# Two expert rows per token, weighted and summed by products with diagonal matrices in PSUM instead of by two vector instructions

## The chip, the cores and the metric

The kernel runs on one core of one Trainium2 chip. The metric is the device time of the core in microseconds (us), from the program's start to its end; less is better. The core has five engines that run their own instruction streams and meet at semaphores: PE (TensorE, matrix products into PSUM), DVE (VectorE), ACT (ScalarE), POOL (GpSimd) and SP (SyncE, which here only starts transfers). The DMA engines move data between HBM and SBUF.

## What is computed

One inference step of a network with two layers, for 128 context tokens and 256 latent tokens of width 1024. Each layer has three kinds of attention heads after one input projection, an output projection and a layer norm, and then a mixture of experts, to which the change belongs. Each token is sent to two of 32 experts, and the two results are added with two weights of that token:

```python
def hier_moe(h, router_group, router_expert, w_gate, w_up, w_down):
    ...
    top_w = jax.nn.softmax(top_v, axis=-1) * g_w
    expert_id = g_sel[:, None] * EXPERTS_PER_GROUP + top_i
    gates = jnp.sum(jax.nn.one_hot(expert_id, N_EXPERTS, dtype=jnp.float32) * top_w[..., None], axis=1).astype(h.dtype)
    ...
    y = jnp.einsum('nef,efd->nd', jax.nn.silu(a) * u * gates[:, :, None], w_down)
    return y.reshape(B, T, D)

def post_norm_residual(x, y, gate, w, b):
    return layer_norm(ALPHA * x + gate * y, w, b)
```

All data are float32.

## The kernel before

The 384 tokens are three tiles of 128 tokens (TILES = 3; tile 0 is the context, tiles 1 and 2 are the latent tokens), with the tokens on the partitions. Each engine runs one hand-written program; a loop over the two layers l holds the stages, and the order of an engine's work is the order of its code.

The expert stage of a layer goes over 16 pairs of experts. For a pair, POOL fetches the rows of its tokens with an indirect DMA (`fetch`, L2154), PE multiplies them with the gate and up weights (L1194) and the down weights (L1218), and POOL scatters the resulting rows to a table `rows` in HBM (`scatter`, L2160; the trace calls it expert_rows). The row of a token's first expert and that of its second stand side by side in the table. Expert pairs with over 64 tokens for one expert need one more round, an "item"; in layer 0 there is one (L1247 to L1283 on PE, L2172 for its scatter), in layer 1 there is none.

When all rows are stored, ACT starts one transfer for each tile (L1583), which brings both rows of the tile's 128 tokens into `gath[t]`, 128 partitions x 2 x 1024. Then DVE does for each tile in turn (L2096 to L2107): three instructions that make (a * w0 + b * w1) * gate2 out of the two rows a and b, the token's two weights `wts[:, 0, t]` and `wts[:, 1, t]` and the row gate2; one that adds ALPHA * x; the moments of the layer norm (L1797, L1803, L1804); and the two instructions of the norm, L1811 and L1813, with the inverse root by POOL (L2147) between them. The end of L1813 signals `ln2_done`.

Who waits for that: in layer 1, the last one, SP stores each tile when its `ln2_done` comes (L840), and the kernel ends with the third store. In layer 0, PE goes on with the next layer's input projection. Its first jobs are, for each tile, 8 transposes of x (L910), which wait for the tile's `ln2_done`, and, after ACT or DVE has copied them out (L1415, L1607), 24 products of 256 columns (L922). SP reloads the attention bias into the buffer of gate2 once all three tiles have their `ln2_done` (L760), and POOL masks it (L2131, L2136).

The weights `wts` come from `weights` on DVE (L1900 to L1907), at the start of the expert stage, before the first of the pairs. The buffer `decay`, 128 partitions x 6 x 128, holds the decay tables of the retention heads; nothing reads it from the retention scores of a layer to the tables of the next. In the expert stage PE writes PSUM banks 0 to 7; the last rows leave banks 5 and 6 with L1493 and L1988 (for an item L1507 and L2019). `ident` is a 128 x 128 identity matrix in SBUF.

Of the kernel before, what the change touches and what calls it, by code (L numbers as in the profile page):

```python
# [22 lines left out]
ALU = mybir.AluOpType  # L23
# [9 lines left out]
TILES = TOKENS // P  # L33
# [351 lines left out]
def build(nc, x_prompt, x_sample, c, cache_na_k, cache_na_v, state_ret, cache_diff_k, cache_diff_v, c_ctx,  # L385
# [12 lines left out]
    with ExitStack() as ctx:  # L398
# [3 lines left out]
        def signal(name, step=0, start=0):  # L402
            s = Signal(ctx.enter_context(nc.semaphore(name)), step, start)
            if start:
                started.append(s)
            return s
# [24 lines left out]
        decay = sb("decay", [P, RET_HEADS, P])  # L431
# [13 lines left out]
        ps = ctx.enter_context(nc.psum_tensor("ps", [P, 8, 512], F32))  # L445

        ident = kc[:, K_ID:K_ID + P]
# [31 lines left out]
        gate2 = [bias[:, :, :, :].rearrange("p h r c -> p (h r c)")[:, k * D:(k + 1) * D] for k in range(2)]  # L479
# [13 lines left out]
        gath = [at(i, 2, D) for i in GATH]  # L493
# [7 lines left out]
        wts = route(2, TILES)  # L501
# [6 lines left out]
        gst = route(8, TILES)  # L508
# [35 lines left out]
        gathered = [signal(f"gathered{i}", 16) for i in range(TILES)]  # L544
# [65 lines left out]
        o_out, o_stored = signal("o_out", 16), signal("o_stored", 1, start=1)  # L610
        var2, rstd2, ln2_done = signal("var2", TILES), signal("rstd2", TILES), signal("ln2_done", TILES)
        combined = signal("combined", TILES)

        dve_link = signal("dve_link", DVE_LINKS)
        pool_link = signal("pool_link", POOL_LINKS)
# [230 lines left out]
        def _(pe):  # L846
# [395 lines left out]
            def item(l, o0, i):  # L1242
# [42 lines left out]
                                           start=(j == 0), stop=(j == 1))  # L1285
                mm.then_inc(o_down.sem, 1)

            for l in range(DEPTH):
                pe.wait_ge(row_act.sem, row_act.at(l, 0))
                pe.wait_ge(row_dve.sem, row_dve.at(l, 0))  # L1290
                for kind, i in FRONT:
                    if l == 0 and kind == "job" and i == JOB_NO["pN", 0, 0]:
                        early_mods(0, 0, CH)
                        early_columns(0)
                    if kind == "job":
                        front_job(l, i)
                    elif kind == "att":
                        if i < N_ATT:
                            scores(l, i)
                        if N_DIFF + 1 < i <= N_ATT:  # L1300
                            probs_T(l, i - 1)
                        if i >= 2:
                            values(l, i - 2)
                        if 1 <= i <= N_DIFF + 1:
                            probs_T(l, i - 1)
                    elif kind == "states":
                        ret_states(l)
                    elif kind == "scores":
                        ret_scores(l, i)
                    elif kind == "out":  # L1310
                        ret_out(l, i)
                mix_T(l, 0)
                mix_T(l, 1)
                out_proj(l, 0)
                mix_T(l, 2)
                out_proj(l, 1)
                rows_logits(l, 0)
                if l + 1 < DEPTH:
                    early_mods(l + 1, 0, 4)
                out_proj(l, 2)  # L1320
                rows_logits(l, 1)
                if l + 1 < DEPTH:
                    early_mods(l + 1, 4, CH)
                rank_products(l, 0, True)
                rows_logits(l, 2)
                if l + 1 < DEPTH:
                    early_columns(l + 1)
                rank_products(l, 1, True)
                rank_products(l, 1, False)
                rank_products(l, 2, True)  # L1330
                first_places(l, (0, 1))
                rank_products(l, 2, False)
                first_places(l, (2,))
                totals(l)
                experts(l)
                wait_alone(pe, items_known, items_known.at(l, 1))
                o1 = items_before(pe, l + 1)
                o0 = items_before(pe, l)
                with pe.If(o1 > o0):
                    with pe.Fori(o0, o1) as i:  # L1340
                        item(l, o0, i)
                pe.wait_ge(row_act.sem, row_act.at(l, PAIRS))
                pe.wait_ge(row_dve.sem, row_dve.at(l, PAIRS))
                pe.wait_ge(o_act.sem, o_act.at(o1, 0))
                pe.wait_ge(o_dve.sem, o_dve.at(o1, 0))

        def drain_to(kind, what, where):

# [239 lines left out]
        def _(dve):  # L1588
# [311 lines left out]
            def weights(l, chain):  # L1900

                dve.wait_ge(gexp_done.sem, gexp_done.at(l, 1))
                chain.link(dve.tensor_reduce(gst[:, 3, :], gtmp, AX.X, ALU.add))
                chain.link(dve.tensor_scalar(gst[:, 5, :], gst[:, 4, :], 1.0, None, ALU.add))
                chain.link(dve.tensor_tensor(gst[:, 5, :], gst[:, 5, :], gst[:, 3, :], ALU.mult))
                chain.link(dve.reciprocal(wts[:, 0, :], gst[:, 5, :]))
                chain.link(dve.tensor_tensor(wts[:, 1, :], wts[:, 0, :], gst[:, 4, :], ALU.mult))  # L1907

            def most(l, chain):

# [110 lines left out]
            for l in range(DEPTH):  # L2021
# [72 lines left out]
                    with dve.Fori(o0, o1) as i:  # L2094
                        item(l, o0, i)
                for t in range(TILES):  # L2096
                    dve.wait_ge(gathered[t].sem, gathered[t].at(l, 16))
                    a, b = gath[t][:, 0, :], gath[t][:, 1, :]
                    if t == 0:
                        dve.wait_ge(gate2_in.sem, gate2_in.at(l, gate2_in.step))  # L2100
                    chain.link(dve.tensor_scalar(a, a, wts[:, 0, t:t + 1], None, ALU.mult))
                    chain.link(dve.scalar_tensor_tensor(a, b, wts[:, 1, t:t + 1], a, ALU.mult, ALU.add))
                    dve.tensor_tensor(a, a, gate2[min(t, 1)], ALU.mult).then_inc(combined.sem, 1)
                    dve.wait_ge(combined.sem, combined.at(l, t + 1))
                    chain.link(dve.scalar_tensor_tensor(x[:, t, :], x[:, t, :], ALPHA, a, ALU.mult, ALU.add))
                    moments(t, chain, var2)
                    normalise(l, t, chain)  # L2107
# [3 lines left out]
        def _(pool):  # L2111
# [37 lines left out]
            def fetch(l, i):  # L2149

                wait_alone(pool, idx_known, idx_known.at(l, 1 if i == 0 else i // GPAIRS + 2))
                if i >= 2:
                    wait_alone(pool, xt_ready, xt_ready.at(l, 2 * (i - 2) + 2))
                pool.indirect_dma_start(xr[i % 2], None, h2d, bass.IndirectOffsetOnAxis(ap=idxu[:, 2 * i + 1:2 * i + 2], axis=0),  # L2154
                                        bounds_check=TOKENS, oob_is_err=False).then_inc(xr_in[i % 2].sem, 16)
# [21 lines left out]
            for l in range(DEPTH):  # L2177
# [48 lines left out]
                wait_alone(pool, h2_stored, h2_stored.at(l, h2_stored.step))  # L2226
                for i in range(4):
                    fetch(l, i)
                for i in range(PAIRS):
                    if i + 4 < PAIRS:  # L2230
                        fetch(l, i + 4)
                    scatter(l, i)
# [10 lines left out]

DVE_LINKS = 205
POOL_LINKS = 19

_INS = ['x_prompt', 'x_sample', 'c', 'cache_na_k', 'cache_na_v', 'state_ret', 'cache_diff_k', 'cache_diff_v', 'c_ctx',
# [24 lines left out]
```

## Times and profile of the kernel before

| what | us |
| --- | --- |
| median of 3 runs | 1266.61 (1263.4 to 1271.74) |
| the profiled execution, its own time | 1269.94 |
| span of its trace | 1268.0 |
| PE busy with products | 1063.1 (84%) |
| DVE busy | 431.6 (34%) |
| ACT busy | 209.4 (17%) |
| POOL busy | 179.3 (14%) |
| last tile's two rows gathered to the end of its norm, see the rows below | 1252.99 to 1262.42 |

The views that are read are the page (a summary of one profiled execution), the chain of work that ended last, the instructions in order of time with merged neighbours, the groups of instructions by line, and tables of stretches with the busy time of each engine and the clock that was granted to TensorE (1.00 is its full 2.4 GHz, 0.50 is 1.2 GHz). A float32 product of the program stands in the trace as two recorded matmuls (the 24 products of L922 for one tile are 48 records); a transpose is one record.

### The profile page before, as it was taken

Reading aid. Unit: us, or ns where it says so; the run is one execution under the profiler, and the core shown is the slowest. Engines: PE = TensorE matmul, PEld = TensorE weight load, DVE = VectorE, ACT = ScalarE, POOL = GpSimd, SP = SyncE. Lnnn points to the kernel's source line nnn. Section 1 sums busy time; section 2 is a strip of 40 time slices with the busy share of each in tenths; the row PEclk is TensorE's granted clock in tenths of the full one; section 3 lists DMA queues with packets and bytes.
Section 4 is the critical chain, followed back from the end, with each engine's and each line's share of the span. In section 5 each row is a group of like instructions: output and inputs, shape, how many; then the busy total and the mean of one; then the engine's idle time right before and its main releaser. Section 6 shows DMA issues by size and latency. Waiting matters only on the chain.

```text
span 1268.0 us, 16407 instructions
## 1 busy us (share of the span) xinstructions
PE 1063.1 (84%) x6576; PEld 711.4 (56%) x6577; DVE 431.6 (34%) x997; ACT 209.4 (17%) x526; POOL 179.3 (14%) x174
## 2 busy tenths in 40 slices
PE   5889999999879998887518999999996999987750
PEld 1755878567755555544206667874785655554420
DVE  0033544258541211110146245443496212111117
ACT  0222324100111110110012223331001111111100
POOL 0350020050111111100004000200401111111001
PEclk8899999998869999989759999999995999999985
DMA  8994222586979999999775321226857899999941
GB/s 350 260 262 148 100 67 79 201 294 231 422 293 418 420 418 419 418 421 418 249 247 163 110 71 67 80 100 236 287 231 276 321 417 420 419 419 419 417 181 78
DMA packets 102703, 343.82 MB, mean 271 GB/s; under 512 B 20242, under 2 KB 61250, under 8 KB 70116
## 3 DMA queue, kind: packets, MB, share of 16 engines
q1 hardware_dynamic: 88256, 314.48, 65.2%
q0 software_dynamic: 12064, 16.74, 4.4%
q10 hardware_dynamic: 2308, 11.54, 2.3%
q8 instruction: 54, 0.88, 0.3%
q14 instruction: 21, 0.17, 0.0%
HBM read 340.87 MB, written 26.16 MB: 289 GB/s over the span
## 4 chain that ended last, share of the span: by engine, by line
PE 62%; DMA 19%; DVE 6%; issue 4%; SPq 4%; POOL 2%; ACT 2%; POOLq 0%; DVEq 0%; ACTq 0%
PE ps L922 15%; PE ps L1194 11%; PE ps L915 8%; DMA ring<-in_exp_w_down 7%; PE ps L1099 7%; PE ps L1218 5%; DMA ring<-in_exp_w_up 5%; SPq L784 4%; DMA arena<-in_exp_w_down 2%; PE ps L1168 2%; PE ps L1161 2%; DMA ring<-in_w_mod 2%; PE ps L864 1%; PE ps L1015 1%; DMA arena<-token_rows,arena 1%
## 5 line engine op out<-in xcount | busy, mean ns | idle before, releaser
L1194 PE MATMUL ps<-ring,arena 128*64 128x256 f32 x1792 | 249.5, 401 | 28.1 <-DMA ring<-in_exp_w_up 15.8
L922 PE MATMUL ps<-ring,arena 128*128 128x256 f32 (+1 forms) x960 | 201.9, 369 | 15.5 <-ACT arena L1415 10.4
L1194 PEld LDWEIGHTS ps<-ring,arena 128*64 128x64 f32 x1792 | 156.5, 144 | 90.9 <-issue 40.4
L922 PEld LDWEIGHTS ps<-ring,arena 128*128 128x128 f32 x960 | 171.3, 196 | 39.6 <-ACT arena L1415 13.0
L1218 PE MATMUL ps<-ring,arena 128*64 128x512 f32 x432 | 121.9, 624 | 15.7 <-DMA ring<-in_exp_w_down 13.2
L1981 DVE TENSOR_TENSOR arena<-arena,ps 128x256 f32<-128x256 f32 x32 | 13.5, 422 | 268.9 <-PE ps L1194 194.4
L915 PE MATMUL ps<-arena,ring 128*128 128x384 f32 x288 | 99.3, 499 | 0.8 <-ACT arena L1420 0.5
L1099 PE MATMUL ps<-ring,arena 128*128 128x256 f32 x384 | 87.5, 390 | 0.0
L1099 PEld LDWEIGHTS ps<-ring,arena 128*128 128x128 f32 x384 | 75.2, 197 | 11.4 <-issue 0.8
L915 PEld LDWEIGHTS ps<-arena,ring 128*128 128x128 f32 x288 | 54.5, 194 | 38.6 <-issue 4.4
L1218 PEld LDWEIGHTS ps<-ring,arena 128*64 128x64 f32 x432 | 36.8, 142 | 69.8 <-issue 66.1
L2154 POOL DMA_INDIRECT arena<-token_rows,arena x32 | 33.4, 1044 | 293.3 <-PE ps L1168 152.1
L1493 ACT ACTIVATE arena<-ps 128x512 f32<-128x512 f32 x32 | 19.1, 597 | 271.8 <-PE ps L1218 271.8
L1168 PE MATMUL ps<-kc,arena 128*128 128x128 f32 x264 | 49.4, 312 | 15.2 <-DMA arena<-token_rows,arena 12.1
L1988 DVE COPY arena<-ps 128x512 f32<-128x512 f32 x32 | 22.1, 691 | 117.1 <-PE ps L1218 117.1
L1194 PE MATMUL ps<-arena 128*64 128x256 f32 x256 | 58.6, 382 | 3.4 <-DMA ring<-in_exp_w_up 2.2
L1168 PEld LDWEIGHTS ps<-kc,arena 128*128 128x128 f32 x264 | 35.6, 196 | 39.7 <-issue 24.2
L864 PE MATMUL ps<-ring,cond 128*32 128x512 f32 x384 | 53.0, 671 | 5.4 <-DMA ring<-in_w_mod 5.4
L2160 POOL DMA_INDIRECT expert_rows<-arena x32 | 32.9, 1028 | 166.7 <-DVE arena L1988 164.9
L1420 ACT ACTIVATE arena<-ps 128x256 f32<-128x256 f32 (+2 forms) x62 | 25.1, 414 | 164.4 <-PE ps L922 116.8
L2147 POOL TENSOR_TENSOR ln_s<-ln_s,kc 128x1 f32<-128x1 f32 x12 | 18.3, 1526 | 155.4 <-DVE ln_s L1804 155.4
L1194 PEld LDWEIGHTS ps<-arena 128*64 128x64 f32 x256 | 33.7, 137 | 11.0 <-issue 4.1
(253 smaller groups left out, 1161.9 us busy)
## 6 DMA issues: line engine op xcount, KB each, us to landing
ring<-in_exp_w_gate SPq DMA_DIRECT2D x58, 1024.0 KB, 25.9
ring<-in_exp_w_up SPq DMA_DIRECT2D x58, 1024.0 KB, 25.7
ring<-in_exp_w_down SPq DMA_DIRECT2D x56, 1024.0 KB, 27.9
ring<-in_w_mod SPq DMA_DIRECT2D x48, 1024.0 KB, 5.9
ring<-in_w_in SPq DMA_DIRECT2D x24, 1024.0 KB, 13.3
arena<-in_exp_w_down SPq DMA_DIRECT2D x10, 1024.0 KB, 28.6
ring<-in_w_out SPq DMA_DIRECT2D x8, 1024.0 KB, 12.8
arena<-in_exp_w_gate SPq DMA_DIRECT2D x8, 1024.0 KB, 25.4
```

The source lines that it names most:

```text
L784: sp.dma_start(dst, src).then_inc(ring_full[place].sem, 16)
L864: mm = pe.matmul(ps[32 * g:32 * g + 32, bank, 0:512], cond[:, ch, :], weights[:, 512 * g:512 * g + 512], start=(ch == 0), stop=(ch == CH - 1))
L915: mm = pe.matmul(out[:, 0:TOKENS], w[:, ch, :], hT[:, ch, :], start=(ch == 0), stop=(ch == CH - 1))
L922: mm = pe.matmul(out[:, 0:w], hT[:, ch, where * P:(where + 1) * P], unit(l, name)[:, ch, 0:w], start=(ch == 0), stop=(ch == CH - 1))
L1099: mm = pe.matmul(ps[:, 2 * t + u // 2, (u % 2) * UCOL:(u % 2 + 1) * UCOL], mixed(ch, t), unit(l, name)[:, ch, :], start=(ch == 0), stop=(c ...
L1161: mm = pe.matmul(ps[:, IDX_BANK[k], 2 * e:2 * e + 4], gsel[:, j, e:e + 2, :].rearrange("p e s -> p (e s)"), tab[:, j, i, :], start=(j == 0 ...
L1168: mm = pe.transpose(ps[:, 7, k * P:(k + 1) * P], src[:, 4 * b + k::CH], ident)
L1194: mm = pe.matmul(ps[64 * w:64 * w + 64, 2 * (i % 2) + kind, 0:FF], xgT[i % 2][:, ch, w * SLOTS:(w + 1) * SLOTS], weights[:, ch * FF:(ch + ...
L1218: mm = pe.matmul(ps[64 * w:64 * w + 64, 5 + n, :], hidT[i % 2][:, j, 64 * w:64 * w + 64], weights[:, j * D + n * 512:j * D + (n + 1) * 512 ...
L1420: act.activation(dst, job_view(j, n, dst), ACT.Copy, scale=RET_SCALE if kind == "rkT" else 1.0)\
L2154: pool.indirect_dma_start(xr[i % 2], None, h2d, bass.IndirectOffsetOnAxis(ap=idxu[:, 2 * i + 1:2 * i + 2], axis=0), bounds_check=TOKENS, o ...
L2160: pool.indirect_dma_start(rows, bass.IndirectOffsetOnAxis(ap=idxu[:, 2 * i:2 * i + 1], axis=0), yb[i % 2], None, bounds_check=ROWS - 1, oo ...
```

## The change

The weighted sum of the two rows moves from DVE to PE. POOL builds, in each layer, six diagonal matrices from the identity, one for each tile and expert rank, with the tokens' weights on the diagonal, and puts them in `decay`, which is free by then. A product of such a matrix with the gathered rows scales each token's row by its weight; PE adds the second expert's product to the first in PSUM. For each tile this is 4 products of 128 x 128 by 128 x 512, into banks 2t and 2t + 1. DVE then multiplies the sum out of PSUM with gate2, one instruction in place of three.

```diff
+            def both_experts(l, t):
+                pe.wait_ge(gathered[t].sem, gathered[t].at(l, 16))
+                for n in range(2):
+                    for k in range(2):
+                        mm = pe.matmul(ps[:, 2 * t + n, :], decay[:, 2 * t + k, :], gath[t][:, k, n * 512:(n + 1) * 512],
+                                       start=(k == 0), stop=(k == 1))
+                mm.then_inc(both_ready.sem, 1)
...
                 pe.wait_ge(o_act.sem, o_act.at(o1, 0))
                 pe.wait_ge(o_dve.sem, o_dve.at(o1, 0))
+                pe.wait_ge(scales_ready.sem, scales_ready.at(l, 1))
+                for t in range(TILES):
+                    both_experts(l, t)
...
-                chain.link(dve.tensor_tensor(wts[:, 1, :], wts[:, 0, :], gst[:, 4, :], ALU.mult))
+                dve.tensor_tensor(wts[:, 1, :], wts[:, 0, :], gst[:, 4, :], ALU.mult).then_inc(wts_ready.sem, 1)
...
                 for t in range(TILES):
-                    dve.wait_ge(gathered[t].sem, gathered[t].at(l, 16))
-                    a, b = gath[t][:, 0, :], gath[t][:, 1, :]
+                    a = gath[t][:, 0, :]
                     if t == 0:
                         dve.wait_ge(gate2_in.sem, gate2_in.at(l, gate2_in.step))
-                    chain.link(dve.tensor_scalar(a, a, wts[:, 0, t:t + 1], None, ALU.mult))
-                    chain.link(dve.scalar_tensor_tensor(a, b, wts[:, 1, t:t + 1], a, ALU.mult, ALU.add))
-                    dve.tensor_tensor(a, a, gate2[min(t, 1)], ALU.mult).then_inc(combined.sem, 1)
+                    dve.wait_ge(both_ready.sem, both_ready.at(l, t + 1))
+                    dve.tensor_tensor(a.rearrange("p (a b) -> p a b", a=2), ps[:, 2 * t:2 * t + 2, :],
+                                      gate2[min(t, 1)].rearrange("p (a b) -> p a b", a=2), ALU.mult).then_inc(combined.sem, 1)
...
                 for i in range(4):
                     fetch(l, i)
+
+                wait_alone(pool, wts_ready, wts_ready.at(l, 1))
+                for t in range(TILES):
+                    for k in range(2):
+                        ins = pool.tensor_scalar(decay[:, 2 * t + k, :], ident, wts[:, k, t:t + 1], 1.0, ALU.mult, ALU.mult)
+                ins.then_inc(scales_ready.sem, 1)
```

On PE the place is the end of layer 0 and the start of layer 1. Before, after the item's down products (L1283), the transposes of x come next:

```order
L1283 MATMUL ps<-ring,arena 64x512 x8
L1340 REGISTER_ALU
L1340 COMPARE_AND_BRANCH
L1339 UNCONDITIONAL_BRANCH
L1344 REGISTER_ALU
L910 MATMUL ps<-kc,x 128x128 x8
L922 MATMUL ps<-ring,arena 128x256 x24
```

Now the 12 products with the diagonal matrices stand ahead of them (the lines of this kernel are 2 to 13 higher there):

```order
L1285 MATMUL ps<-ring,arena 64x512 x8
L1353 REGISTER_ALU
L1353 COMPARE_AND_BRANCH
L1352 UNCONDITIONAL_BRANCH
L1357 REGISTER_ALU
L1297 MATMUL ps<-arena,decay 128x512 x12
L912 MATMUL ps<-kc,x 128x128 x8
L924 MATMUL ps<-ring,arena 128x256 x24
```

What moved: all three tiles' products are queued ahead of tile 0's transposes, which open the next layer. At the end of layer 1 the same 12 products are PE's last work.

On DVE the place is the end of a layer, here tile 0 and the first instruction of tile 1. Before:

```order
L2101 TENSOR_SCALAR arena<-arena 128x1024
L2102 SCALAR_TENSOR_TENSOR arena<-arena 128x1024
L2103 TENSOR_TENSOR arena<-arena,bias 128x1024
L2105 SCALAR_TENSOR_TENSOR x<-x,arena 128x1024
L1797 BN_STATS ln_s<-x 128x6 x2
L1803 BN_AGGR ln_s<-ln_s 128x2
L1804 TENSOR_SCALAR ln_s<-ln_s 128x1
L1811 SCALAR_TENSOR_TENSOR x<-x,ln_s,arena 128x1024
L1813 SCALAR_TENSOR_TENSOR x<-x,ln_s,arena 128x1024
L2101 TENSOR_SCALAR arena<-arena 128x1024
```

Now:

```order
L2117 TENSOR_TENSOR arena<-ps,bias 128x1024
L2120 SCALAR_TENSOR_TENSOR x<-x,arena 128x1024
L1813 BN_STATS ln_s<-x 128x6 x2
L1819 BN_AGGR ln_s<-ln_s 128x2
L1820 TENSOR_SCALAR ln_s<-ln_s 128x1
L1827 SCALAR_TENSOR_TENSOR x<-x,ln_s,arena 128x1024
L1829 SCALAR_TENSOR_TENSOR x<-x,ln_s,arena 128x1024
L2117 TENSOR_TENSOR arena<-ps,bias 128x1024
```

What moved: two instructions of each tile are gone, and the one with gate2 (in the buffer bias) reads PSUM.

On POOL the place is the start of the expert stage. The fetches of the first four pairs are followed by the six matrices, and then by the fifth fetch:

```order
L2239 MEMSET arena 128x2048
L2169 DMA arena<-token_rows,arena 128x1024 x4
L2248 TENSOR_SCALAR decay<-kc,arena 128x128 x6
L2169 DMA arena<-token_rows,arena 128x1024
L2175 DMA expert_rows<-arena 769x1024
```

What moved: before, the five fetches stood together; the six instructions of 128 x 128 are between the fourth and the fifth.

## Rows read from the trace of the kernel before

**Rows 1.** The page's chain of work that ended last, its shares by engine.
```profile
PE 62%; DMA 19%; DVE 6%; issue 4%; SPq 4%; POOL 2%; ACT 2%; POOLq 0%; DVEq 0%; ACTq 0%
```

**Rows 2.** End of layer 1 in time order: start us, us, engine, line, instruction [idle before].
```profile
1229.45 1.31 ACTq L1583 DMA_DIRECT2D arena<-expert_rows  x3
1234.26 0.75 DVE L2101 TENSOR_SCALAR arena<-arena 128x1024 f32<-128x1024 f32 x1 [8.50 <-DMA arena<-expert_rows]
1235.05 1.28 DVE L2102 SCALAR_TENSOR_TENSOR arena<-arena 128x1024 f32<-128x1024 f32 x1
1236.37 1.22 DVE L2103 TENSOR_TENSOR arena<-arena,bias 128x1024 f32<-128x1024 f32 x1
...
1243.64 0.75 DVE L2101 TENSOR_SCALAR arena<-arena 128x1024 f32<-128x1024 f32 x1
...
1261.14 1.28 DVE L1813 SCALAR_TENSOR_TENSOR x<-x,ln_s,arena 128x1024 f32<-128x1024 f32 x1 [0.51 <-POOL ln_s L2147]
```

**Rows 3.** End of layer 0 and start of layer 1 in time order.
```profile
651.21 0.75 DVE L2101 TENSOR_SCALAR arena<-arena 128x1024 f32<-128x1024 f32 x1 [14.59 <-DMA arena<-expert_rows]
...
659.38 1.28 DVE L1813 SCALAR_TENSOR_TENSOR x<-x,ln_s,arena 128x1024 f32<-128x1024 f32 x1 [0.53 <-POOL ln_s L2147]
...
660.81 1.95 PE L910 MATMUL ps<-kc,x 128*128 128x128 f32 x8 [24.93 <-DVE x L1813]
...
664.99 12.81 PE L922 MATMUL ps<-ring,arena 128*128 128x256 f32 x48 [2.23 <-ACT arena L1415]
...
668.75 1.28 DVE L1813 SCALAR_TENSOR_TENSOR x<-x,ln_s,arena 128x1024 f32<-128x1024 f32 x1 [0.52 <-POOL ln_s L2147]
...
677.63 1.35 PE L910 MATMUL ps<-kc,x 128*128 128x128 f32 x8
...
681.31 10.60 PE L922 MATMUL ps<-ring,arena 128*128 128x256 f32 x48 [2.34 <-ACT arena L1415]
```

**Rows 4.** Layer 1's last down products in time order; each half of the array has its own.
```profile
1221.85 0.59 PE L1218 MATMUL ps<-ring,arena 128*64 128x512 f32 x1
...
1222.28 0.59 PE L1218 MATMUL ps<-ring,arena 128*64 128x512 f32 x1
...
1225.08 0.69 DVE L1988 COPY arena<-ps 128x512 f32<-128x512 f32 x1 [3.94 <-PE ps L1218]
```

**Rows 5.** Stretches: us, then busy us (instructions) of PE, PEld, DVE, ACT, POOL, PEclk, DMA, GB/s.
```profile
643.00:651.00 8.00, 0.00 (x0) 0.00 (x0) 0.00 (x0) 0.00 (x0) 0.00 (x0) 0.50 1.10 367
...
665.00:669.00 4.00, 4.00 (x10) 3.19 (x11) 3.26 (x7) 0.00 (x0) 1.52 (x1) 0.50 0.00 0
669.00:671.00 2.00, 2.00 (x10) 1.73 (x9) 1.96 (x3) 0.08 (x1) 0.00 (x0) 0.88 0.00 0
671.00:678.00 7.00, 7.00 (x36) 6.20 (x34) 6.31 (x8) 0.86 (x3) 1.51 (x1) 1.00 0.00 0
...
1234.00:1244.00 10.00, 0.00 (x0) 0.00 (x0) 8.88 (x11) 0.00 (x0) 1.54 (x1) 0.50 0.45 192
```

**Rows 6.** Stretches as in Rows 5: the transfers while DVE works on tile 0.
```profile
651.00:655.00 4.00, 0.00 (x0) 0.00 (x0) 3.69 (x4) 0.00 (x0) 0.00 (x0) 0.50 1.01 422
655.00:657.00 2.00, 0.00 (x0) 0.00 (x0) 1.97 (x3) 0.00 (x0) 0.00 (x0) 0.50 0.13 53
...
1238.00:1240.00 2.00, 0.00 (x0) 0.00 (x0) 1.97 (x3) 0.00 (x0) 0.00 (x0) 0.50 0.24 98
```

**Rows 7.** The instructions of line L1823: count, ns least/median/most.
```profile
L1823 DVE TENSOR_TENSOR arena<-ps,ring x4: 1217/1220/1224, 295.5 to 934.0; 128x1024 f32<-128x1024 f32 x4
```

**Rows 8.** The instructions of L2181; then in time order, start of layer 0's experts.
```profile
L2181 POOL TENSOR_SCALAR dnw<-dnw,lamk x2: 477/484/490, 72.7 to 678.0; 128x256 f32<-128x256 f32 x2
...
368.86 0.16 DVE L1907 TENSOR_TENSOR arena<-arena 128x3 f32<-128x3 f32 x1
...
376.05 1.34 POOL L2154 DMA_INDIRECT arena<-token_rows,arena  x1 [10.77 <-PE ps L1168]
392.76 0.99 POOL L2154 DMA_INDIRECT arena<-token_rows,arena  x1 [15.38 <-DVE arena L1968]
```

More of the change, by code:

```diff
@@ L612, in build @@
         combined = signal("combined", TILES)
+        wts_ready, scales_ready = signal("wts_ready", 1), signal("scales_ready", 1)
+        both_ready = signal("both_ready", TILES)
         dve_link = signal("dve_link", DVE_LINKS)
@@ L2242, in _ @@
                 assert chain.n == POOL_LINKS, chain.n
-DVE_LINKS = 205
+DVE_LINKS = 198
 POOL_LINKS = 19
```

## Prediction

> **What bounds the kernel now.** I read the chain of work that ended last first: over the whole span it lies on PE for 62% and on transfers for 19%, on DVE for only 6% [rows 1]. The change touches DVE, so its worth depends on the few places where DVE is in the chain, and these I read in order of time. There are two. At the end of layer 1 nothing but DVE works: tile 0's gathered rows land at 1234.26, DVE goes through three tiles almost without a gap, and its last instruction ends at 1261.14 + 1.28 = 1262.42 [rows 2]; the store follows, and is not changed. At the end of layer 0 PE has been idle for 24.93 us when it starts on the transposes of tile 0, at 660.81, released by the end of DVE's L1813 on that tile [rows 3]. From there PE is the bound: tile 1's x is ready at 668.75 + 1.28 = 670.03, and PE comes to it at 677.63. So in layer 0 only DVE's time for tile 0 counts, and in layer 1 its time for all three.
>
> **What is removed.** Up to the multiplication with gate2, a tile costs DVE 1236.37 - 1234.26 = 2.11 us (L2101 and L2102) [rows 2]; in layer 0 it is the same two instructions, and I take 2.11 too. The rest of a tile, from L2103 to the next tile's L2101, takes 1243.64 - 1236.37 = 7.27 us and stays. The multiplication now reads PSUM: the kernel has that form elsewhere, with one input in PSUM and one in SBUF, at 1.22 us [rows 7], against 1.22 from SBUF [rows 2]. It costs nothing more.
>
> **What is added on PE.** No row shows a float32 product with 128 rows, 128 columns of weights and 512 moving columns. The nearest is L1218, 512 columns on one half of the array, with the other half busy beside it. Its records on one half start 1222.28 - 1221.85 = 0.43 us apart at full clock [rows 4], and a product is two records, so 0.86 us. A tile has 4 products, 8 records: 3.44 us. The matrices' weight loads lie beside the running product, as they do for L922: 48 records of 256 columns took 10.60 us [rows 3], 0.22 each, half of the 0.43 that 512 columns take, so the width of the weights adds nothing. From below, the price cannot be under one record per product, 1.72 us; from above it is the half clock, 6.88. After the last record DVE needs some time: 8 records on that half end with one that starts at 1221.85 + 6 x 0.43 = 1224.43, and DVE starts at 1225.08 [rows 4], 0.22 us after that record's 0.43.
>
> The clock decides between 3.44 and 6.88. PE has nothing to do before the gathered rows land: the granted clock is 0.50 in the 8 us before them in layer 0, and stays at 0.50 at the end of layer 1 [rows 5]. Where PE starts anew in layer 0, it runs L922 at 0.50 for 665 to 669, and at a mean of 0.88 over the next 2 us [rows 5]; that is full clock from about 669.5, 4.5 us after its start at 664.99. The same comes from the two totals, 12.81 for the first 48 records and 10.60 for the next [rows 3]: 2.2 us lost, 4.4 us at half. So in its first 4.5 us PE does 2.25 us of the 3.44, the other 1.19 run at full clock, and with the 0.22 the first tile's sum is ready **5.9 us** after its rows have landed. In place of 2.11, that is **+3.8 us** for tile 0.
>
> Here a page of the Trainium skill can be weighed against the rows. TensorE: Matmul & The Clock Gate, section Back-to-back issue gap, gives about 216 ns for a matmul of 512 columns at full rate, and with that alone the four products would take 0.86 us. The rows of this kernel show 0.86 us for one float32 product, four times as much. The same skill's FP8 and Floating Point Precision, section TensorE Precision Notes, gives four passes for true float32, with which the trace agrees. By the first figure alone the sum would come out as the rival of cheap products below; by the second it is mine.
>
> **The sum at the end of layer 1.** Tile 0 +3.8. Tiles 1 and 2: their rows have landed before 1240, since the transfers fade out in 1238 to 1240 [rows 6], so PE goes on without a wait at full clock and has tile 1 done 5.7 + 3.44 = 9.1 us after the landing and tile 2 at 12.6. DVE comes to them at 5.9 + 7.27 = 13.2 and 20.4. They are hidden, and DVE gains 2.1 on each. 3.8 - 2.1 - 2.1 = **-0.4 us**.
>
> **The sum at the end of layer 0.** Tile 0's x comes 3.8 later, so the transposes could start at 664.6 in place of 660.81. But all 12 products stand ahead of them on PE: 651.2 + 5.7 + 2 x 3.44 = 663.8, just before 664.6, with rows that are all there by 657 [rows 6]. So they are hidden by DVE's work on tile 0, with less than 1 us to spare. And they leave PE at full clock. From the transposes to L922 it was 664.99 - 660.81 = 4.18 us for tile 0 and 681.31 - 677.63 = 3.68 for tile 1, and L922 took 12.81 against 10.60 [rows 3]: 0.5 + 2.2 = 2.7 us given back. 3.8 - 2.7 = **+1.1 us**. Tile 1's x comes at 670.03 + 3.8 - 2.1 = 671.7, PE wants it at 678.7; tile 2 is further from the path still. SP's reload of the bias comes 0.4 earlier, and changes nothing by itself.
>
> **What is added on POOL.** The nearest row is a tensor_scalar of 128 x 256 at 0.48 us [rows 8]; for 128 x 128 I bound one by 0.24 and 0.48, six by 1.5 and 2.9. Their weights are known at 369.0, the fourth fetch ends at 377.4, the fifth starts at 392.76 [rows 8]: 15 us of POOL standing idle hide them, and cost 0. Without that cover a fetch would be up to 2.9 us late in each layer. The link that DVE no longer waits for is nothing beside them.
>
> -0.4 + 1.1 = +0.7. The profiled execution took 1269.94 us, so 1270.6 on its scale; the median shown is 3.3 lower, and on its scale I predict **1267.3 us**: no measurable change. What a measurement can tell from no change is about 1%, 12.7 us.
>
> **The rivals.**
> - *The clock rises within the first product.* All at full clock, tile 0 takes 3.66 and costs +1.55: layer 1 gives 1.55 - 4.2 = -2.65, layer 0 1.55 - 2.7 = -1.15. Together -3.8: 1262.8. Against it are 4.4 us at half in the one fresh start that I have costed [rows 3, 5].
> - *Cheap products*, one pass each, 4 x 0.21 at full clock, 1.7 at half, 1.9 with the rest: -0.2 in layer 0 with nothing given back, -4.4 in layer 1, 1262.0. Against it is the spacing of the records [rows 4].
> - *The clock is not given back.* PE falls to half clock again in the pauses between the transposes and L922, and the 2.7 are missing: +3.4, 1270.0. For it: the pauses are there, 2.2 us [rows 3]. Against it: between tile 0 and tile 1 the same pause of 2.3 left L922 at 10.60.
> - *Slower: PE's queue at the start of layer 1.* The transposes of tile 0 wait behind the products of tiles 1 and 2, whose x nobody needs yet. If the clock stays at half through all 24 records, these take 24 x 0.86 = 20.6 us and end at 671.8; tile 0's x is there at 665.7. The transposes start 11.1 us later than before, nothing is given back, and layer 1's end adds 5.0 - 4.2 = +0.8: +11.9, 1278.5. It decides from the point where the half clock lasts over 8.6 us, for then 10.3 + 4.3 us of PE pass DVE's 6.9 + 0.2 + 7.5. The spare of less than 1 us speaks for it, the 4.4 us against.
> - *The matrices are not hidden*, by 2.9 us in each layer: +6.5, 1273.1. Against it, 15 us of cover.
>
> **How the numbers follow.** My forecast, -1 to +2.5 around +0.7, gets 0.66; the early clock 0.09; cheap products 0.02; no clock given back 0.12; the queue 0.06; matrices in the way 0.02; something unnamed 0.03. The three runs shown spread over 8 us, so a median of the new kernel can lie 2 or 3 us off. The range of 1261.5 to 1272.5 holds the first four with that spread and leaves out the last three and the edges. Faster by over 1% needs 1254, which no case reaches: 0.02. Slower by over 1% needs 1279.3; the queue stands just below it, so half of it and the unnamed: 0.06. Same: 0.92.
>
> **What would show it.** In the new profile: 8 records for the first tile in about 5.7 us, with a granted clock of 0.50 for most of it; DVE's multiplication starting 5.9 us after the rows land, and 13.2 and 20.4 for the next ones; PE's last product at the end of layer 0 ending before DVE's norm of tile 0; L922 of tile 0 at 10.6 us; six POOL instructions under 0.5 us each before the fifth fetch. I am wrong if the products are at half clock into tiles 1 and 2, if the transposes wait for products and not for x, or if a product's records are not 0.43 us apart at full clock.

## The result

| | before | changed |
| --- | --- | --- |
| median, us | 1270.40 (17 runs, 1262.66 to 1274.21) | 1275.44 (17 runs, 1270.04 to 1277.06) |
| ratio | | 1.0038, 95% interval 1.0024 to 1.0053 |
| span of the profiled execution | 1268.0 | 1271.4 |
| PE busy, us | 1063.1 | 1091.7 |
| DVE busy, us | 431.6 | 417.8 |
| DVE's start on tile 0's gate2 after the rows landed, layer 0 / layer 1, us | 2.11 / 2.11 | 5.99 / 6.36 |
| tile 1's transposes after that landing, layer 0, us | 26.42 | 29.39 |
| landing of tile 0's rows to the end of the last norm, layer 1, us | 28.16 | 28.21 |

The change makes the kernel slower by 0.38% (3 to 7 us). That is within the 1% that I had called no change, but it is clear of the noise of 17 runs, it is more than the +0.7 us of the sum, and 1275.44 lies above the range. The second measurement of the same kernel (`after_again`, below) gave 1.0012 (0.9992 to 1.0032), which by itself does not exclude that nothing is lost. The ratios below leave out three slow executions that stand far off all others (two of the kernel before, 1844 and 1615 us, and one of e2, 4433 us).

In order of time, the end of layer 0 in the changed kernel reads as follows (start us, us, engine, line, instruction, count, [idle before]). It answers to [rows 3].

```profile
648.11 12.75 PE L1297 MATMUL ps<-arena,decay 128*128 128x512 f32 x24 [15.42 <-DMA arena<-expert_rows]
...
654.10 1.23 DVE L2117 TENSOR_TENSOR arena<-ps,bias 128x1024 f32<-128x1024 f32 x1 [20.67 <-PE ps L1297]
...
661.62 1.13 PE L912 MATMUL ps<-kc,x 128*128 128x128 f32 x8 [0.75 <-DVE x L1829]
...
665.38 12.28 PE L924 MATMUL ps<-ring,arena 128*128 128x256 f32 x48 [2.64 <-ACT arena L1431]
...
677.50 1.35 PE L912 MATMUL ps<-kc,x 128*128 128x128 f32 x8
...
681.19 10.60 PE L924 MATMUL ps<-ring,arena 128*128 128x256 f32 x48 [2.34 <-ACT arena L1431]
```

Tile 0's sum is ready at 654.10, 5.99 us after the landing at 648.11. All 24 records end 12.75 after it, the transposes come at 13.51, and they wait for x, 0.75 us, not for products. The first block of L924 takes 12.28 us, and not 10.60 as the next one. The end of layer 1 in the same view answers to [rows 2]:

```profile
1237.88 13.12 PE L1297 MATMUL ps<-arena,decay 128*128 128x512 f32 x24 [9.50 <-DMA arena<-expert_rows]
...
1244.24 1.23 DVE L2117 TENSOR_TENSOR arena<-ps,bias 128x1024 f32<-128x1024 f32 x1 [15.12 <-PE ps L1297]
...
1251.53 1.22 DVE L2117 TENSOR_TENSOR arena<-ps,bias 128x1024 f32<-128x1024 f32 x1
...
1258.77 1.22 DVE L2117 TENSOR_TENSOR arena<-ps,bias 128x1024 f32<-128x1024 f32 x1
...
1264.81 1.28 DVE L1829 SCALAR_TENSOR_TENSOR x<-x,ln_s,arena 128x1024 f32<-128x1024 f32 x1 [0.51 <-POOL ln_s L2162]
```

Tiles 1 and 2 follow 7.29 and 7.24 us after the tile ahead of them, with no wait for PE; before, tile 1 followed at 9.38 [rows 2]. What the two gain, 4.2 us, tile 0 loses. The stretches of the changed kernel (busy us and count of PE, PEld, DVE, ACT, POOL, then the granted clock, DMA share, GB/s) show why tile 0 is dear:

```profile
648.00:652.00 4.00, 3.89 (x5) 1.85 (x6) 0.00 (x0) 0.00 (x0) 0.00 (x0) 0.50 1.00 416
652.00:653.00 1.00, 1.00 (x3) 0.26 (x2) 0.00 (x0) 0.00 (x0) 0.00 (x0) 0.71 0.09 33
653.00:660.00 7.00, 7.00 (x18) 3.17 (x17) 5.29 (x7) 0.00 (x0) 1.47 (x1) 1.00 0.00 0
...
1242.00:1243.00 1.00, 1.00 (x2) 0.34 (x1) 0.00 (x0) 0.00 (x0) 0.00 (x0) 0.50 0.00 0
1243.00:1250.00 7.00, 7.00 (x18) 3.06 (x17) 5.29 (x7) 0.00 (x0) 1.32 (x1) 0.99 0.00 0
```

The products begin at 1.2 GHz and are at 2.4 GHz from about 652.6 and 1243.0, 4.5 and 5.1 us after their start. The rule of the Trainium skill's TensorE: Matmul & The Clock Gate, section What's actually happening, that the engine is throttled by default and activity releases it, agrees with these rows.

### The profile page after: what moved, and what is told of

The parts are those of the page before. It is cut to its first block, busy times and chain, and to the rows that moved or that the text cites. A ratio compares the mean times of both kernels' runs of the same rounds, so it can differ in the third digit from the quotient of the medians.

```text
span 1271.4 us, 16506 instructions
## 1 busy us (share of the span) xinstructions
PE 1091.7 (86%) x6624; PEld 723.2 (57%) x6625; DVE 417.8 (33%) x985; ACT 209.3 (16%) x526; POOL 183.5 (14%) x186
## 4 chain that ended last, share of the span: by engine, by line
PE 63%; DMA 19%; DVE 5%; issue 4%; SPq 4%; POOL 2%; ACT 2%; POOLq 0%; DVEq 0%; ACTq 0%
PE ps L924 15%; PE ps L1196 12%; PE ps L917 8%; DMA ring<-in_exp_w_down 7%; PE ps L1101 7%; PE ps L1220 5%; DMA ring<-in_exp_w_up 5%; SPq L786 3%; DMA arena<-in_exp_w_down 2%; PE ps L1170 2%; PE ps L1163 2%; DMA ring<-in_w_mod 2%; PE ps L866 1%; PE ps L1017 1%; DMA arena<-token_rows,arena 1%
## 5 line engine op out<-in xcount | busy, mean ns | idle before, releaser
L924 PE MATMUL ps<-ring,arena 128*128 128x256 f32 (+1 forms) x960 | 204.3, 372 | 15.4 <-ACT arena L1431 10.8
L924 PEld LDWEIGHTS ps<-ring,arena 128*128 128x128 f32 x960 | 173.0, 197 | 40.0 <-ACT arena L1431 13.2
L1297 PE MATMUL ps<-arena,decay 128*128 128x512 f32 x48 | 25.9, 704 | 24.9 <-DMA arena<-expert_rows 24.9
```

Of the source, the lines that this page charges most:

```text
L924: mm = pe.matmul(out[:, 0:w], hT[:, ch, where * P:(where + 1) * P], unit(l, name)[:, ch, 0:w], start=(ch == 0), stop=(ch == CH - 1))
L1297: mm = pe.matmul(ps[:, 2 * t + n, :], decay[:, 2 * t + k, :], gath[t][:, k, n * 512:(n + 1) * 512], start=(k == 0), stop=(k == 1))
```

## The experiments

My theory after the result (A): tile 0's sum takes 6 us or more on PE in place of 2.1 on DVE, at the end of both layers; in layer 1 the other two tiles pay this back, in layer 0 nothing does but a little of the clock. Rivals: B, POOL's matrices disturb the expert stage; C, more PE work at this place shifts the falls of PE's clock (its granted clock going from 1.00 to 0.50 for some microseconds) into stretches that ran at full clock before. C was suggested by this stretch of the next layer's attention, in the kernel before and then in the changed one (the mean granted clock is 1.00 and 0.84; PE is busy nearly throughout in both):

```profile
712.00:734.00 22.00, 19.60 (x80) 11.18 (x79) 7.93 (x20) 6.59 (x17) 0.00 (x0) 1.00 0.15 52
```

```profile
712.00:734.00 22.00, 19.60 (x64) 10.51 (x62) 6.81 (x17) 6.08 (x15) 0.00 (x0) 0.84 0.13 48
```

These quantities tell the kernels apart, in us and read in order of time. "Sum": DVE's start on gate2 after tile 0's rows landed, in layer 0 and in layer 1. "x": tile 0's transposes after that landing. "Block": the first 48 records of L922 behind them. "Tile 1": tile 1's transposes after the landing. "Middle": from the third block's start to the landing in layer 1. "End": from there to the end of the last norm. "Clock" is the mean granted clock in 712 to 734 us of the trace; that stretch is the same time in every trace and not quite the same work, since tile 0's rows of layer 0 land between 648.1 and 653.7. "Ratio" is the time against that of the kernel before, measured beside it (17 executions of each for the changed kernel; below, 29 of the kernel before, 12 of each variant, 6 of e4 and of e8). The intervals behind the ratios are 95% intervals.

| kernel | sum | x | block | tile 1 | clock | middle | end | ratio to before |
| --- | --- | --- | --- | --- | --- | --- | --- | --- |
| before | 2.11 / 2.11 | 9.60 | 12.81 | 26.42 | 1.00 | 537.8 | 28.16 | |
| changed | 5.99 / 6.36 | 13.51 | 12.28 | 29.39 | 0.84 | 542.0 | 28.21 | 1.0038 |
| after_again | 6.24 / 6.64 | 13.75 | 12.29 | 29.65 | 0.92 | 538.5 | 28.50 | 1.0012 |
| e1 | 2.11 / 2.11 | 9.61 | 12.34 | 25.96 | 1.00 | 538.7 | 28.17 | 0.9991 |
| e2 | 2.11 / 2.11 | 9.61 | 13.17 | 26.38 | 1.00 | 538.0 | 28.16 | 0.9993 |
| e3 | 3.81 / 5.51 | 11.33 | 12.04 | 26.97 | 0.84 | 538.7 | 27.37 | 0.9993 |
| e4 | 2.11 / 2.11 | 12.36 | 10.60 | 26.48 | 0.92 | 535.9 | 23.96 | 0.9951 |
| e5 | 2.10 / 6.56 | 9.60 | 12.82 | 26.43 | 1.00 | 537.8 | 28.41 | 1.0011 |
| e6 | 6.31 / 2.11 | 13.82 | 12.28 | 29.71 | 0.84 | 539.2 | 28.16 | 1.0032 |
| e8 | 2.11 / 2.11 | 9.60 | 10.52 | 24.37 | 0.92 | 539.0 | 23.95 | 0.9934 |

**e1: the matrices alone.** POOL's part of the diff stays, PE's goes, and DVE has its three instructions back.

```diff
+def by_products(l, t):
+    return False
...
                 for t in range(TILES):
-                    both_experts(l, t)
+                    if by_products(l, t):
+                        both_experts(l, t)
...
                     if t == 0:
                         dve.wait_ge(gate2_in.sem, gate2_in.at(l, gate2_in.step))
+                        dve.wait_ge(scales_ready.sem, scales_ready.at(l, 1))
```

> Only POOL's six diagonal matrices of each layer are added to the kernel before (DVE waits for them at the end of the layer, where they are long done); the sum of the two rows stays on DVE. Theory A, that the loss comes from tile 0's sum taking 6 us on PE in place of 2.1 on DVE: no change, within 1 us, and the six instructions as in the changed kernel, 2.3 us in all. Rival B, that POOL's work in the expert stage disturbs DVE or the fetches: +2 to +5 us, with the fifth fetch later than before.

The ratio is 0.9991 (0.9974 to 1.0009). In order of time on POOL:

```profile
373.66 1.34 POOL L2187 DMA_INDIRECT arena<-token_rows,arena  x1 [10.85 <-PE ps L1178]
375.05 2.29 POOL L2266 TENSOR_SCALAR decay<-kc,arena 128x128 f32<-128x128 f32 x6
390.38 1.07 POOL L2187 DMA_INDIRECT arena<-token_rows,arena  x1 [13.05 <-DVE arena L1993]
```

The six instructions take 2.29 us, 0.38 each, and the fifth fetch starts 16.72 us after the fourth, as before (392.76 - 376.05 = 16.71 [rows 8]). B, which wanted at least 2 us, falls.

**e2: unused products at the same place.** As e1, and on PE:

```diff
+                pe.wait_ge(gathered[0].sem, gathered[0].at(l, 16))
+                for i in range(7):
+                    pe.matmul(ps[:, i % 6, :], decay[:, 0, :], decay[:, 1:5, :].rearrange("p a b -> p (a b)"),
+                              start=True, stop=True)
```

> As e1, and PE makes 7 products of 512 columns in each layer from the time when tile 0's rows have landed; nobody reads them, and the sum stays on DVE. They should take about 8.5 us and end before tile 0's x is ready (9.6 us after the landing), so they are on no path. Theory A: no loss; a gain of 0.5 us (the transposes of tile 0 at full clock) to 2.7 (the first 48 records of the next projection too). Rival C, that 5 us are lost because more PE work at this place shifts the clock's falls into later stretches: +2 us or more, with stretches at 0.50 after 700 us that the kernel before does not have.

The ratio is 0.9993 (0.9973 to 1.0014). No loss is seen, the middle is 538.0, and the clock of 712 to 734 is 1.00: 8.7 us of work on PE at this place cost nothing that shows, and C, which wanted at least 2 us, has nothing from this kernel. But the gain of up to 2.7 us did not come either. PE in order of time:

```profile
652.28 8.69 PE L1370 MATMUL ps<-decay 128*128 128x512 f32 x14 [15.19 <-DMA arena<-expert_rows]
661.88 1.14 PE L920 MATMUL ps<-kc,x 128*128 128x128 f32 x8 [0.91 <-DVE x L1842]
665.65 13.17 PE L932 MATMUL ps<-ring,arena 128*128 128x256 f32 x48 [2.63 <-ACT arena L1444]
```

The transposes ran at full clock (1.14 in place of 1.95), and then the block took 13.17 us, longer than without any products ahead of it. Tile 1 came no earlier. Here the clock had fallen in the pause ahead of the block: its mean was 1.00 in 663 to 664 and 0.51 in 664 to 665, with PE at rest. This is the first sight of the step that failed in my prediction.

**e3: the clock held up to the landing.** The changed kernel, and ahead of its products:

```diff
                 pe.wait_ge(scales_ready.sem, scales_ready.at(l, 1))
+                for i in range((16, 9)[l]):
+                    pe.matmul(ps[:, i % 4, :], decay[:, 0, :], decay[:, 1:5, :].rearrange("p a b -> p (a b)"),
+                              start=True, stop=True)
                 for t in range(TILES):
                     both_experts(l, t)
```

> The changed kernel, with unused products of 512 columns (16 in layer 0, 9 in layer 1) between PE's last expert work and the landing of the rows, so that PE comes to tile 0's products at full clock. Theory A: tile 0's sum takes 3.7 us in place of 6.0 and 6.4, DVE starts 2.3 to 2.7 us earlier in both layers, and the kernel is 4 to 5.5 us faster than the changed one, that is 0 to 1 us slower or faster than the kernel before. If the clock is not what makes the sum dear, it stays where the changed kernel is, +5.

The ratio is 0.9993 (0.9975 to 1.0012), so no loss is left that shows. In layer 0 the sum took 3.81 us, as forecast:

```profile
652.04 10.57 PE L1297 MATMUL ps<-arena,decay 128*128 128x512 f32 x24 [1.29 <-DMA arena<-expert_rows]
```

In layer 1 it took 5.51. The unused products ended 1.94 us before the rows landed there, and the clock went while PE was already back at work (stretches):

```profile
1236.00:1237.00 1.00, 0.51 (x1) 0.36 (x2) 0.00 (x0) 0.00 (x0) 0.00 (x0) 0.84 0.97 410
1237.00:1238.00 1.00, 1.00 (x2) 0.34 (x1) 0.00 (x0) 0.00 (x0) 0.00 (x0) 0.50 1.00 426
1238.00:1240.00 2.00, 2.00 (x4) 0.75 (x3) 0.00 (x0) 0.00 (x0) 0.00 (x0) 0.50 1.05 442
```

So the clock makes 2.2 to 2.4 us of tile 0's price in layer 0 and 0.9 to 1.1 of it in layer 1 here, and the traces add up to 2.4 (tile 1) + 0.8 (end) = 3.2 us against the changed kernel. The expectation of 4 to 5.5 was too high by the layer 1 part.

**e4: tile 0 by DVE, tiles 1 and 2 by products.** The functions are those of the two kernels; a rule says who sums which tile.

```diff
+def by_products(l, t):
+    return t > 0
...
                 for t in range(TILES):
-                    both_experts(l, t)
+                    if by_products(l, t):
+                        both_experts(l, t)
```

> The change for tiles 1 and 2 alone, in both layers; tile 0's sum stays on DVE. Theory A: the end of layer 1 is 4.2 us shorter than in the kernel before; at the end of layer 0 the 16 records start when tile 1's rows have landed, about 2 us after tile 0's, and end 11 us after tile 0's landing, so the transposes come 1 to 2 us late and get at most that back: -2 to -4 us against the kernel before. Rival C (work on PE at this place costs by itself): +1 or more.

The ratio is 0.9951 (0.9931 to 0.9970): 3.8 to 8.8 us faster than the kernel before. The expectation of 2 to 4 lies at the lower edge of that; the trace shows 4.1 us of it at the two ends. PE at the end of layer 0, and DVE's last instruction of layer 1, whose tile 0 landed at 1233.65:

```profile
656.07 10.03 PE L1305 MATMUL ps<-arena,decay 128*128 128x512 f32 x16 [17.89 <-DMA arena<-expert_rows]
665.93 1.04 PE L920 MATMUL ps<-kc,x 128*128 128x128 f32 x8
669.62 10.60 PE L932 MATMUL ps<-ring,arena 128*128 128x256 f32 x48 [2.65 <-ACT arena L1440]
```

```profile
1256.33 1.28 DVE L1838 SCALAR_TENSOR_TENSOR x<-x,ln_s,arena 128x1024 f32<-128x1024 f32 x1 [0.51 <-POOL ln_s L2180]
```

The end is 23.96 us, 4.20 less than before: both later tiles gain their 2.1, and nothing is paid for it there. In layer 0 the transposes waited behind tile 2's products, 12.36 in place of 9.60 (my slower rival's mechanism, at 2.8 us), but here the block ran at 10.60, and tile 1 came as before.

**after_again: the changed kernel once more.** No edit.

> The changed kernel once more, for a second profile and on the same chip as the next three. Its first profile has three stretches at half clock that the kernel before did not pay in the same way: the first 48 records after tile 0's transposes (12.28 us in place of 10.60), and 718 to 724, which the kernel before ran at full clock. If these falls belong to the change, the second profile has both again. If they are where the clock happens to fall in an execution, the second has them elsewhere or not at all, and between the third L924 block and the landing of layer 1's rows it takes 538 us, as in the kernel before, and not 542. The end of layer 0, from tile 0's landing to tile 1's transposes, should again be 29.4 us against 26.4, and the end of layer 1 28.2.

The ratio is 1.0012 (0.9992 to 1.0032). Tile 1 comes at 29.65, the block takes 12.29, the end 28.50: the loss at the two ends is there again. The middle is 538.5 and not 542.0, so 3.5 us of the first profile's span were that execution's. Most of them arise before the expert stage of layer 1: POOL's first fetch of that stage starts 279.4 us after the third block in the first profile, 276.5 in the second, and 276.1 in the kernel before.

The fall of the clock between 712 and 734 is not so simple. It is there again, shorter (0.92). Over all 14 profiles, it is absent in the four in which DVE makes the whole sum of layer 0 (before, e1, e2, e5), and present in 8 of the 10 others (e9 and e10, below, have it in one of two each). But in large part it is a fall that moves and not one that is added: the six profiles without it have one a little earlier, between 696 and 705, in or just ahead of the third block, and of the eight with it only the first profile of the changed kernel and e6 have that earlier one too. So it goes with the timing there, though not in each execution and not with PE's extra work alone (e2). What it costs is small: among the other nine profiles of the table, the middle is 535.9 to 539.2 us with it and 537.8 to 538.7 without.

**e5 and e6: one layer each.** Against e4, the rule alone changes.

```diff
-    return t > 0
+    return l == DEPTH - 1
```

> The change in layer 1 alone; in layer 0 DVE makes the sum as before. Theory A: tile 0 +4.3, tiles 1 and 2 -2.1 each: +0.1 us, no change. If the loss of 5 us came from the end of the kernel it would be seen here.

```diff
-    return t > 0
+    return l == 0
```

> The change in layer 0 alone; in layer 1 DVE makes the sum as before. Theory A: all of the loss, +3 us from the late transposes of tile 0 less what the clock gives back, and up to +5 if the falls of the clock in the next layer's projections belong to it. With e5 it should add up to the changed kernel's +5.

e5 1.0011 (0.9991 to 1.0030), e6 1.0032 (1.0012 to 1.0051). The loss stands in e6: its interval excludes that nothing is lost, and its tile 1 comes 3.3 us later than before. e5's interval includes that nothing is lost, and its trace shows +0.25 us at the end. Their losses add to 0.43%; the changed kernel's two measurements gave 0.38 and, on the chip of e5 and e6, 0.12, each to within about 0.2.

**e8: tile 2's products behind tile 0's transposes.** As e4, and at the start of layer 1:

```diff
                     if kind == "job":
                         front_job(l, i)
+                        if l and JOBS[i] == ("xT", 0, 1):
+                            both_experts(l - 1, 2)
...
                 for t in range(TILES):
-                    both_experts(l, t)
+                    if by_products(l, t) and (t < 2 or l == DEPTH - 1):
+                        both_experts(l, t)
```

> As e4 (tile 0's sum on DVE, tiles 1 and 2 by products), and at the end of layer 0 tile 2's products stand behind tile 0's transposes on PE, in the time in which ACT copies these out. In e4 the transposes of tile 0 wait for tile 2's products, about 2 us. Here they should start 9.6 us after tile 0's landing, as in the kernel before, and the kernel should be 0.5 to 1.5 us faster than e4: -5 to -7 us against the kernel before.

The ratio is 0.9934 (0.9908 to 0.9960), the lowest of all: 5 to 12 us faster than the kernel before. Whether it is faster than e4, the intervals leave open.

```profile
661.79 1.13 PE L920 MATMUL ps<-kc,x 128*128 128x128 f32 x8 [0.75 <-DVE x L1840]
662.76 3.60 PE L1305 MATMUL ps<-arena,decay 128*128 128x512 f32 x8
666.20 10.52 PE L932 MATMUL ps<-ring,arena 128*128 128x256 f32 x48
676.56 1.35 PE L920 MATMUL ps<-kc,x 128*128 128x128 f32 x8
680.24 12.29 PE L932 MATMUL ps<-ring,arena 128*128 128x256 f32 x48 [2.33 <-ACT arena L1442]
```

The products fill the time in which ACT copies the transposes out. Tile 1 comes at 24.37, 2.0 us earlier than in the kernel before. But the fall of the clock, absent from the first block, is in the second one (12.29).

**e9 and e10: does a pause on PE make the fall?** Up to here every kernel in which PE paused 0.75 to 0.91 us between products and the first transposes and then 2.6 us until the block had the fall in that block, and the two without one of these pauses, e4 the first and e8 the second, had not. e9 is the changed kernel with one more unused product in layer 0:

```diff
                     both_experts(l, t)
+                if l == 0:
+                    pe.matmul(ps[:, 6, :], decay[:, 0, :], decay[:, 1:5, :].rearrange("p a b -> p (a b)"),
+                              start=True, stop=True)
```

> The changed kernel with one more product of 512 columns, unused, in layer 0 behind tile 2's products, in the pause of 0.75 us in which PE waits for tile 0's x. So far the first block of the next projection had a fall of the clock in it (12.0 to 13.2 us) in all kernels in which PE paused 0.75 to 1.3 us between products and transposes, and none (10.5 and 10.6) in e4 and e8, where it did not pause. If the pause makes the fall: the block takes 10.6 us, and tile 1's transposes start 27.8 us after tile 0's landing in place of 29.5. If not: 12.3 and 29.5.

> The same kernel as e9_pause_filled, for a second profile: the same block is 10.6 us if the pause makes the fall, 12.3 if not; if the two profiles differ, it is neither.

e10 is e4 with tile 2 of layer 0 left to DVE:

```diff
-    return t > 0
+    return t == 1 or (t == 2 and l == DEPTH - 1)
```

> As e4, but in layer 0 tile 2's sum stays on DVE too, so that PE has tile 1's products alone; they end about 8.2 us after tile 0's landing, 1.4 us before the transposes. If the pause makes the fall, the first block takes 12.3 us or more in place of the 10.6 of e4; if not, 10.6. The end of layer 1 stays at 24.0 us.

> The same kernel as e10_pause_left, for a second profile: 12.3 us or more if the pause makes the fall, 10.6 if not; if the two differ, it is neither.

One run each: 1273.90 and 1273.80 for e9, 1268.21 and 1267.30 for e10, beside 1273.62 for the kernel before. PE in e9, in e10 and in its second profile:

```profile
664.50 1.02 PE L1363 MATMUL ps<-decay 128*128 128x512 f32 x2
665.41 1.13 PE L912 MATMUL ps<-kc,x 128*128 128x128 f32 x8
669.18 12.29 PE L924 MATMUL ps<-ring,arena 128*128 128x256 f32 x48 [2.64 <-ACT arena L1434]
```

```profile
663.32 1.13 PE L920 MATMUL ps<-kc,x 128*128 128x128 f32 x8 [0.46 <-DVE x L1838]
667.09 10.60 PE L932 MATMUL ps<-ring,arena 128*128 128x256 f32 x48 [2.64 <-ACT arena L1440]
```

```profile
663.15 1.13 PE L920 MATMUL ps<-kc,x 128*128 128x128 f32 x8 [0.67 <-DVE x L1838]
666.91 12.28 PE L932 MATMUL ps<-ring,arena 128*128 128x256 f32 x48 [2.64 <-ACT arena L1440]
```

With the first pause filled the fall stays (12.29; 12.28 in the second profile), and with a pause the same kernel has it in one execution and not in the other. So the first, short pause alone does not decide.

The 14 profiles do show a tendency that none of these runs was made for. Between the last product and the next block PE does nothing but the 8 transposes and waits for their copies. Over the first three blocks of the next projection in all profiles (leaving out the first blocks of the kernel before, e1 and e5, which start with the clock still at 0.50, and that of e8, which has products right ahead of it), this stretch without products was 2.8 to 3.7 us ahead of 20 blocks, of which 5 took over 12 us and the others 10.6; 3.8 to 4.1 us ahead of 6, of which 3 took over 12; and 4.2 to 5.6 us ahead of 12, of which 11 did. In the changed kernel it is 665.38 - 660.86 = 4.52 us ahead of tile 0's block and 3.5 ahead of tile 1's. A longer stretch without products goes with more falls; that it is their cause, and what decides in a single execution, is not shown.

## Why the prediction was wrong

- **The bound, right.** In layer 0 only tile 0's time on DVE counted, in layer 1 all three (e5, e6).
- **What is removed, right.** Tiles 1 and 2 follow 2.1 us faster each; e4's end shows it clean, -4.20. The gate2 instruction from PSUM took 1.23 us, as [rows 7].
- **A float32 product as two records of 0.43 us, right.** The 16 records of tiles 1 and 2 go at that pace, 7 us of the 12.75 in all; cheap products fall. So does the clock that rises within the first product.
- **Tile 0's sum at 5.9 us, a little low.** It took 5.99 to 6.64 us in the six layer ends of the changed kernel, its second profile, e5 and e6, because the half clock lasted up to 5.7 us and not 4.5 (the longest is in layer 1 of the second profile, whose products start at 1235.82 and whose granted clock is 0.50 in 1240 to 1241 and 0.71 in 1241 to 1242). That is +0.05 to +0.3 at the end of layer 1, where I had -0.4.
- **The queue on PE, right.** The products of tiles 1 and 2 ended 0.75 us before tile 0's x was there; I had 0.8.
- **The matrices, right.** 2.28 us in the gap of 15, and e1 shows no cost.
- **The clock given back, the step that failed.** I took the transposes and the whole first block at full clock, 0.5 + 2.2 = 2.7 us. The transposes and the wait behind them gave 0.4, the block 0.5 (12.28 for 12.81): it began at full clock and then fell to 0.50 for some microseconds, where the block of [rows 5] began at 0.50 and rose. Stretches of the changed kernel:

```profile
665.00:667.00 2.00, 1.62 (x6) 1.40 (x7) 1.73 (x4) 0.24 (x1) 1.19 (x1) 0.81 0.00 0
667.00:669.00 2.00, 2.00 (x7) 1.55 (x6) 1.56 (x2) 0.00 (x0) 0.33 (x1) 0.50 0.00 0
669.00:671.00 2.00, 2.00 (x9) 1.75 (x8) 1.97 (x2) 0.20 (x1) 0.00 (x0) 0.84 0.00 0
```

With 0.9 given back in place of 2.7, the end of layer 0 is +3.0 and not +1.1, and the sum +3.0 to +3.6 and not +0.7. This is my rival of the clock that is not given back, at +3.4, to which I had given 0.12. What I had put against it was that tile 1's block ran at 10.60 after a pause of the same length. Two things were wrong with that. The pauses were not the same: with the transposes counted in, the stretch without products is 3.5 us for tile 1 and became 4.5 for tile 0. And one block was no measure of how often the clock falls: tile 1's block itself took 12.29 in 3 of the 14 profiles (e1, e3, e8), the first of them a kernel in which PE does nothing new:

```profile
679.49 12.29 PE L932 MATMUL ps<-ring,arena 128*128 128x256 f32 x48 [2.34 <-ACT arena L1440]
```

Tile 0's block took 10.5 or 10.6 in only 3 of the 11 profiles in which PE came to the transposes at full clock.
- **The range.** It was put around the median shown, 1266.61, which came from 3 runs; over 17 runs the kernel before has 1270.40. These 3.8 us are the larger part of why the result lies outside: the same range around 1270.40 would have ended at 1276.3 and held 1275.44. That the count was 3 runs was known, and the range allowed 2 or 3 us for it. From 1270.40 the forecast would have been 1271.1, and 1275.44 is 4.3 above it. The traces show a loss of 3.0 to 3.6 us in all (3.0 to 3.3 at the end of layer 0, 0.05 to 0.3 at the end of layer 1), so 2.3 to 2.9 of the 4.3. A loss of 3.0 to 3.6 lies inside the interval of the second measurement (-1 to 4 us) and at the lower edge of that of the first (3 to 7 us). Where the rest of the first measurement's 5 us comes from, and whether the fall in 712 to 734 adds a microsecond to it on the average, no run settles.

## What to carry to other kernels

Moving vector work to an idle PE was worth what it saved on the tiles that PE could finish behind other work, and cost its full latency, at half clock, on the first tile, which somebody waits for; so leave the first tile on the engine that is awake and move the later ones. The rest of such work can stand behind the transposes of the next stage in the queue and not ahead of them: in e8's trace that brought tile 1 2.1 us earlier than in e4's, though the two measured times do not tell them apart. And a gain that hangs on PE's clock being up across pauses should enter a sum with the share of executions in which it was seen (3 of 11 here), not in full.

## What was not expected of the hardware

- The clock can be lost after PE has come back to work: in e3 PE paused 1.94 us at a granted clock of 1.00, started, and was at 0.50 within 1 us, for about 3 us.
- A fall of the clock 60 us downstream of the edit, in attention code that it doesn't touch, in 8 of 10 profiles with products for the sum of layer 0 and in none of 4 without; the six that lack it have a fall about 20 us earlier instead.
- The block after a pause of 2.64 us took 10.60 us in one execution of e10 and 12.28 in the next, so one profile does not tell whether such a block pays for a fall of the clock. Over all profiles such blocks paid more often the longer PE had been without products (5 of 20, 3 of 6, 11 of 12).
- Products ahead of a pause did not help the block behind it in e2: 13.17 us, against 12.81 with PE idle for 25 us before the transposes.
